# A four-layer hybrid decoder step on eight cores: three convolution heads ahead of v in the first pass, and five smaller reorderings

## What is computed

```python
for l in range(4):
    h = rmsnorm(x, pre_g[l])
    u, v, z_a, p, z_b, xc, bg, cg, z_c = split(h @ w_in[l])        # 1024 -> 6400 columns
    vn  = rmsnorm(v, v_g[l])                                       # A: chunks of 128, 6 heads
    a   = u * (tril(w_s[h]) @ vn + b_s)
    d   = trailing_mean(p, 2/4/8/16) - p                           # B: 4 groups of 128 channels
    b   = (d @ w_pg) * pool_scale
    c   = bg * conv3(cg * xc)                                      # C: depthwise, width 3, 6 heads
    mix = concat(a * silu(z_a), b * silu(z_b), c * silu(z_c))
    x   = x + rmsnorm(mix @ w_out[l], post_g[l])
```

## Time and profile before

| | us |
|---|---|
| median of 3 runs | 2166.12 |
| the three runs | 2033.6, 2166.12, 2173.4 |
| the profiled execution | 2033.48 |
| its span, slowest core | 2032.3 |
| spans of the eight cores | 2029.0 to 2032.3 |
| granted TensorE clock, mean | 0.996 to 0.999 |

### The profile page before, as it was taken

The page is one execution under the profiler, slowest core; times in us unless marked ns, Lnnn a source line. Parts: engine busy times, 40 slices in busy tenths (PEclk is TensorE's granted clock), DMA queues, the critical chain, the costliest instruction groups (busy, mean ns, idle before and its releaser), DMA issues.

```text
span 2032.3 us, 37323 instructions; the slowest of 8 cores (2029.0 to 2032.3 us)
## 1 busy us (share of the span) xinstructions
PE 2004.1 (99%) x12305; PEld 1185.9 (58%) x12305; DVE 1174.8 (58%) x1935; ACT 630.7 (31%) x1566; POOL 382.7 (19%) x752
## 2 busy tenths in 40 slices
PE   7999999999999999999999999999999999999998
PEld 4555565576566466557656546656755655664673
DVE  4654764575665475476575556547657544653763
ACT  4232332323323232232332332323333222231331
POOL 3211310221211120131131122013013111101300
PEclk9999999999999999999999999999999999999999
DMA  9999797689798875839969857595987974656662
GB/s 187 215 193 193 167 204 105 171 131 193 178 181 139 161 157 94 138 115 181 183 169 177 137 156 145 96 140 135 194 186 168 160 144 137 115 87 144 115 122 75
DMA packets 157099, 309.53 MB, mean 152 GB/s; under 512 B 78192, under 2 KB 83568, under 8 KB 155504
## 3 DMA queue, kind: packets, MB, share of 16 engines
q0 software_dynamic: 47376, 174.64, 54.5%
q1 hardware_dynamic: 109392, 132.25, 23.7%
q10 hardware_dynamic: 144, 0.26, 0.0%
HBM read 409.48 MB, written 55.99 MB: 229 GB/s over the span
## 4 chain that ended last, share of the span: by engine, by line
PE 93%; DMA 4%; DVE 1%; issue 1%; POOL 0%; SPq 0%; ACT 0%; DVEq 0%; POOLq 0%; ACTq 0%
PE ps L590 61%; PE ps L706 23%; PE ps L558 7%; DMA hd<-sb_hout 2%; DMA sb_b_bc<-b_sp 1%; PE ps L829 1%; DMA sb_ring<-w_in 1%; DMA sb_xs<-x_p 1%; PE ps L684 1%; PE ps L747 0%; DVE sb_pw L410 0%; DVE sb_mix L414 0%; POOL sb_stats L425 0%; DVE sb_vn L414 0%; ACT sb_scr L406 0%
## 5 line engine op out<-in xcount | busy, mean ns | idle before, releaser
L590 PE MATMUL ps<-sb_hT,sb_ring 128*128 128x384 bf16 (+1 forms) x8448 | 1324.7, 317 | 6.6 <-DVE sb_mix L414 3.0
L590 PEld LDWEIGHTS ps<-sb_hT,sb_ring 128*128 128x128 bf16 x8448 | 823.1, 98 | 471.6 <-issue 12.1
L406 ACT ACTIVATE sb_scr<-ps 128x384 f32<-128x384 f32 (+3 forms) x665 | 370.8, 562 | 1047.2 <-PE ps L590 494.2
L706 PE MATMUL ps<-sb_wout,sb_mix 128*128 128x512 bf16 x2144 | 464.7, 379 | 0.0
L706 PEld LDWEIGHTS ps<-sb_wout,sb_mix 128*128 128x128 bf16 x2144 | 209.9, 98 | 251.6
L356 POOL DMA_DIRECT2D sb_ring<-w_in x284 | 153.3, 543 | 973.1 <-PE ps L590 626.2
L414 DVE SCALAR_TENSOR_TENSOR sb_scr<-sb_pw,sb_convw,sb_scr 128x384 f32<-128x384 f32 (+1 forms) x336 | 182.0, 542 | 145.8 <-ACT sb_ccarry L406 109.5
L410 DVE TENSOR_TENSOR sb_scr<-ps,sb_scr 128x384 f32<-128x384 f32 (+1 forms) x288 | 151.8, 531 | 118.2 <-PE ps L829 91.4
L414 DVE SCALAR_TENSOR_TENSOR sb_hout<-sb_xs,sb_stats,sb_pre_bc 128x1024 bf16<-128x1024 f32 x62 | 79.6, 1285 | 189.3 <-POOL sb_stats L425 168.7
L558 PE MATMUL ps<-sb_ring,sb_hT 128*128 128x512 bf16 (+1 forms) x1088 | 178.8, 326 | 0.9 <-DMA sb_ring<-w_in 0.9
L410 DVE TENSOR_TENSOR sb_mix<-sb_scr 128x384 bf16<-128x384 f32 (+1 forms) x288 | 160.2, 556 | 30.7 <-DVE sb_scr L410 0.9
(11 more groups left out here) (55 smaller groups left out, 521.5 us busy)
## 6 DMA issues: line engine op xcount, KB each, us to landing
sb_ring<-w_in POOLq DMA_DIRECT2D x273, 512.0 KB, 10.9
xd<-sb_xs SPq DMA_DIRECT2D x51, 512.0 KB, 3.1
sb_xs<-xd SPq DMA_DIRECT2D x51, 512.0 KB, 11.8
sb_xs<-x_p SPq DMA_DIRECT2D x32, 512.0 KB, 15.2
sb_wout<-w_out POOLq DMA_DIRECT2D x32, 512.0 KB, 13.0
hd<-sb_hout SPq DMA_DIRECT2D x62, 256.0 KB, 4.2
sb_ring<-w_in POOLq DMA_DIRECT2D x11, 1024.0 KB, 9.9
y_p<-sb_xs SPq DMA_DIRECT2D x16, 512.0 KB, 2.9
```

Of the source, the lines that this page charges most:

```text
L406: return emit(ACT, lambda a: a.activation(out=out, in_=in_, func=func, scale=scale, **kw), reads=reads, writes=writes)
L590: ins = pe.matmul(bank(b, N), lhsT=wa.ap[:, k, :], rhs=hT[:, k, j0 * 128:j0 * 128 + N], start=(k == 0), stop=(k == 7))
L706: ins = pe.matmul(bank(b + half), lhsT=mix[:, k, j * 128:(j + 1) * 128], rhs=wout[:, k, half * 512:(half + 1) * 512], start=(k == 0), stop ...
```

## The change

1. Pass 0 runs convolution heads 0 to 2 (N_FRONT) ahead of v. Their six units move in the ring list behind p; w_sp, its mask product and the bias are handled in the hooks of these heads. SyncE no longer waits for v1. w_sp is staged in vn rows 4 and 5 rather than mix rows 10 and 11. The w_out pieces go to other hooks: heads 1 and 2 of the front, v tiles 3 and 5, a heads 1, 3, 5, and convolution head 3.
2. At the start the first weight unit is issued after the first norm, icnt, the setup constants and w_pg later. Rows 3 to 5 are copied to hT by VectorE. All pooling operations of pass 0 come after the front.
3. Next rows: in pass 0 the x tiles of pass 1 are asked for at v tiles 0 to 3 instead of 3 to 5, and hout has three buffers instead of two.
4. The bias table of the samples is gone; the operation repeats each of 8 values 16 times by its access pattern. b_bc is 3 KB a partition instead of 6, and the transfer half as large.
5. In the passes of group 2 the hooks take three pooling entries after v tiles 0 to 3, none after the last, none at head 0, two at the heads behind it.
6. In out_last each half's sum is waited for by its own token; eps is added to the first half's sum at once; sum and power follow.

```diff
-NHO = 2
+NHO = 3
...
+            if (g, l) == (0, 0):
+                k = len(units) - 12
+                units = units[:2] + units[k:k + 2 * N_FRONT] + units[2:k] + units[k + 2 * N_FRONT:]
+            pending.extend(units)
...
-            act(hT[:, :, j * 128:(j + 1) * 128], pb.rearrange("p (k t) -> p k t", k=8), AF.Copy,
-                reads=[bank_res[b]], writes=[R_hT[j]])
+            if on_dve:
+                dve_copy(hT[:, :, j * 128:(j + 1) * 128], pb.rearrange("p (k t) -> p k t", k=8),
+                         reads=[bank_res[b]], writes=[R_hT[j]])
...
-                dve_tt(scr[:, tm + half, :], bank(b + half), post_bc[:, half * 512:(half + 1) * 512], ALU.mult,
-                       reads=[bank_res[b + half], R_stat[sa[half]], R["post_bc"]], writes=[R_scr[tm + half]])
+                summed = R_stat[sa[half]].w
+                emit(DVE, lambda v, half=half: v.tensor_tensor(
+                    out=scr[:, tm + half, :], in0=bank(b + half), in1=post_bc[:, half * 512:(half + 1) * 512],
+                    op=ALU.mult),
+                     reads=[bank_res[b + half], R["post_bc"]], writes=[R_scr[tm + half]], extra=[summed])
+                if half == 0:
+                    emit(POOL, lambda q: q.tensor_scalar(out=c0, in0=c0, scalar1=EPS, scalar2=None, op0=ALU.add),
+                         reads=[R_stat[sa[0]]], writes=[R_stat[sa[0]]])
...
-                        bv = b_bc[:, k, h * 128:(h + 1) * 128]
+                        bv = b_bc[:, h * 128:(h + 1) * 128]
+                        if k == 1:
+                            bv = bv[:, 0:ST].unsqueeze(2).to_broadcast([128, ST, SB])
...
-                later_pop(2 if h == 0 else 3)
+                if g < 2:
+                    later_pop(2 if h == 0 else 3)
+                elif h > 0:
+                    later_pop(2)
...
-                ring_try_alloc()
                 warm_up()
                 nr(0)
+                ring_try_alloc()
                 nr(1)
-                ring_try_alloc()
                 sl.append(load_x(0, 4))
                 tj(0, 8)
                 nr(2)
-                load_wpg(0, 1, d_wpg[0])
                 ring_try_alloc()
...
-                v1 = W0["v1"].res[0].w
-                SP.h.wait_ge(*v1)
-                SP.waited[id(v1[0])] = v1[1]
-                setup_loads()
...
+                wo = list(range(8))
+
+                def hook(c):
+                    if c == 0:
+                        emit(SP, lambda q: q.dma_start(out=w32, in_=w_sp[0]), writes=R_w32, dsem=d_pw[1])
+                        load_b(0)
+                    else:
+                        wout_piece(l, wo.pop(0))
+                    if c == 1:
+                        dve_tt(wmt[:], w32.rearrange("p (a b) -> p a b", a=6),
+                               c32[:, C32_MASKP, :].unsqueeze(1).to_broadcast([128, 6, 128]), ALU.mult,
+                               reads=R_w32 + [R["c32"]], writes=[R["wmt"]])
+                c_phase(g, l, hook, 0, N_FRONT)
+                for gi in range(4):
+                    pool_vec(g, l, gi)
...
-                if j >= 3 or nt - j <= 3:
+                if (j < 4 if pi == 0 else j >= 3 or nt - j <= 3):
                     init_load()
-                later_pop(2 if g == 2 else 1)
+                if g < 2:
+                    later_pop(1)
+                elif j < nt - 1:
+                    later_pop(3)
...
-            c_phase(g, l, hook)
+            c_phase(g, l, hook, 0 if pi else N_FRONT)
```

More of the change, by code:

```diff
@@ L76 @@
 W_UNITS = _w_units()
+N_FRONT = 3
 W_ORDER = [s for u in W_UNITS for s in u]
@@ L175, in build_nc @@
     w_sm = din("w_sm", [DEPTH, 128, 6 * 128])
-    b_sp = din("b_sp", [DEPTH, 128, 2 * 768])
+    b_sp = din("b_sp", [DEPTH, 128, 768])
     w_pg = din("w_pg", [128, DEPTH * 4 * 128])
@@ L237, in build_nc @@
         vstage = sb("vstage", [128, WA], F32)
-        b_bc = sb("b_bc", [128, 2, 768], F32)
+        b_bc = sb("b_bc", [128, 768], F32)
         xs = sb("xs", [128, NX, D], F32)
@@ L388, in build_nc @@
             r0 = 0
+            units = []
             for names in W_UNITS:
@@ L398, in build_nc @@
                 u.slots = sum(x[2] for x in names) // 128
-                pending.append(u)
+                units.append(u)
+            if (g, l) == (0, 0):
+                k = len(units) - 12
+                units = units[:2] + units[k:k + 2 * N_FRONT] + units[2:k] + units[k + 2 * N_FRONT:]
+            pending.extend(units)
             wsched[(g, l)] = d
@@ L491, in load_b @@
         def load_b(l):
-            emit(SP, lambda q: q.dma_start(out=b_bc[:].rearrange("p a b -> p (a b)"), in_=b_sp[l]),
+            emit(SP, lambda q: q.dma_start(out=b_bc[:], in_=b_sp[l]),
                  writes=[R["b_bc"]], dsem=d_par["b"])
@@ L532, in norm_to_hd, with t_job @@
                  dsem=d_hout[o])
-        def t_job(j, s):
+        def t_job(j, s, on_dve=False):
             b = alloc_banks()
@@ L741, in out_last @@
             sa = [alloc_stat(), alloc_stat()]
+            c0 = stats[:, sa[0]:sa[0] + 1]
+            c1 = stats[:, sa[1]:sa[1] + 1]
             ju = alloc_scr()
@@ L857, in a_phase, with c_phase @@
                 hook(h)
-        def c_phase(g, l, hook):
+        def c_phase(g, l, hook, c0=0, c1=6):
             W = wsched[(g, l)]
             sts = GROUPS[g][1]
-            for c in range(6):
+            for c in range(c0, c1):
                 wzc = need(W[("zc", c)])
@@ L968, in run_pass @@
                 nr(2)
-                load_wpg(0, 1, d_wpg[0])
                 ring_try_alloc()
                 sl.append(load_x(0, 5))
+                emit(SP, lambda s_: s_.dma_start(out=icnt[:].rearrange("p a b -> p (a b)"), in_=icnt_d),
+                     writes=[R["icnt"]], dsem=d_icnt)
                 tj(1, 5)
@@ L975, in run_pass @@
                 tj(2, 4)
+                setup_loads()
                 load_vg(0)
@@ L982, in run_pass @@
                 pump()
+                load_wpg(0, 1, d_wpg[0])
                 pb_[1] = p_matmul(g, l, 1, 0)
@@ L992, in run_pass @@
                 for gi in range(4):
-                    pj(gi, 1)
+                    p_job(g, l, gi, 1)
                     release(wsched[(g, l)][("p", gi)])
-                    pool_vec(g, l, gi)
-                    later_pop(2 if gi else 0)
-                v1 = W0["v1"].res[0].w
-                SP.h.wait_ge(*v1)
-                SP.waited[id(v1[0])] = v1[1]
-                setup_loads()
[L1001 to L1004, removed]
+                w32 = vn[:, 4:6, :].rearrange("p k t -> p (k t)").bitcast(F32)
+                R_w32 = [R_vn[4], R_vn[5]]
+                wo = list(range(8))
[3 more added lines that the diff above has]
+                        load_b(0)
+                    else:
+                        wout_piece(l, wo.pop(0))
[5 more added lines that the diff above has]
+                for gi in range(4):
+                    pool_vec(g, l, gi)
             else:
@@ L1012, in run_pass @@
                 pool_phase(g, l, gmaj, hook)
-            wo = list(range(8)) if g == 0 else []
+            if pi:
+                wo = list(range(8)) if g == 0 else []
             init_t = list(GROUPS[pi + 1][0]) if pi < 2 else []
@@ L1054, in hook @@
                     wout_piece(l, wo.pop(0))
-                if c == 1 and (g == 0 or pi == 1) and l + 1 < DEPTH:
+                if c == (1 if pi else N_FRONT) and (g == 0 or pi == 1) and l + 1 < DEPTH:
                     load_pre(l + 1)
```

26 lines of the change are left out of this document (10 added, 16 removed).

## The result

The changed kernel takes 2051.59 us in the median of 6 runs. Against the kernel before the ratio is 1.0085, with a 95% interval of 1.0067 to 1.0103: slower by 0.85%, within the 2% that counts as the same. The profiled execution took 2051.04, its span is 2049.6, that of before 2032.3. The median of before, 2166.12 from three runs and 2100.84 from six, mixes runs near 2034 with runs in which one half of the chip ran at a lower clock, so it can't be set beside 2051.59; the ratio leaves those runs out.

A forecast was written before the change was run, and what follows sets the result against it. TensorE was busy 2004.1 of 2032.3 us, with DMA engines also full in the first pass. 2032.3 + 5.0 (first pass) + 11.7 (group 2) - 1.2 (tail) = 2047.8 span, given as 2050; own range 2042 to 2058, reaching to 2190.

The forecast's parts named there:

- The first pass: First pass: output projection starts 3.3 us later, waiting for w_out, plus 1.7 us of lower clock: +5.0 us.
- the group 2 passes: Passes 2, 5 and 8: 2.2 us net delay plus 1.7 us clock, 3.9 per pass, +11.7; last layer 0.
- what is given back in group 2: Head 0 of group 2: its pooling pair is gone, so the 0.73 us wait goes; net 2.9 - 0.7 = +2.2 us.
- The clock in group 2: Passes 2, 5, 8: lower TensorE clock after each 3.3 us wait, 1.7 us per pass, bounds 0 and 2.5.
- Last vn in group 2: Group 2 v phase: four more VectorE pooling operations ahead of the last vn delay it by 2.9 us.
- Last w_out piece: First pass: eighth piece, queued behind v0 and v1 of pass 1, lands at 172.0 instead of 163.2; bounds 168.5 and 177.
- The row transposes: Pass 1's transposes, issued up to 12 us sooner, hardly take any engine share; otherwise w_out lands nearer 177, sum 5 us higher.
- TensorE's arrival: First pass: TensorE reaches the output projection at 156.6 instead of 168.66, then waits 15 us for w_out.
- Clock behind the wait: Output projection of first pass: lower clock after the w_out wait costs 1.7 us, bounds 0 and 2.5.
- Tail: End of kernel: earlier eps and one operation fewer, -0.8 - 0.4 = -1.2 us; bounds -0.7 and -1.2.
- The range: Case as summed 2042 to 2058, chance 0.45; range reached to 2190 because two of three earlier times lay 6.5% higher.
- The intended gains of the first pass: Earlier start and 8.1 us of removed waits; w_out in time gives -12.1 (2033, chance 0.13); with group 2's gain 2018, 0.12.

The follow-up runs named there:

- the old hooks: Changed kernel with group 2's pooling hooks as before the change (two per v tile and at head 0, three at heads 1 and 2): span 2034.5 us, ratio 1.0011.
- the new hooks alone: Kernel before with only the new group 2 pooling hooks: span 2047.2 us, ratio 1.0077.
- norm elsewhere: Changed kernel with group 2's carried-over row norm run behind head 1 of the a phase instead of in the p phase: span 2036.7 us, ratio 1.0021.
- the run with the late piece: Kernel before with only pass 0's eighth w_out piece issued at convolution head 3 instead of 2: span 2041.1 us, timed runs 2041.73 and 2042.31.

## Why the total came out close, and which steps of the prediction failed

The cause, the places and the direction were as forecast: 2047.8 for the span, measured 2049.6, and +0.8% against 1.0085. That the total is so close is partly luck, as misses of opposite sign cancel. The first pass cost 3.8 us instead of 5.0, the group 2 passes 14.7 instead of 11.7. Point by point:

- **The step that failed: what is given back in group 2.** The prediction followed the list of 28 pooling entries only to the last vn, credited what head 0 no longer does, and put pass 11 at 0. What is pushed back it put at nothing without a reason. Head 3 now has two entries left, and its group matmul waits 1.39 us for them in all four passes of group 2, 5.6 us in all. Nearly all of the 1.6 us of pass 11 is this wait. The runs with the old hooks and with the new hooks alone show that the hooks bring it.
- **The clock in group 2.** 1.7 us were charged for each of three waits, 5.1 in all. The profiled core paid in passes 2 and 8 and not in pass 5, 2.7 us in all (13.1 measured, less three times 3.5 of waits). So the forecast of 11.7 was 3 x 2.2 + 3 x 1.7; the terms measured, 3 x 2.1 + 4 x 1.39 + 2.7, come to 14.6 of the 14.7. The overcharge of 2.4 us hid part of the missed 5.6.
- **Last vn in group 2.** Right: the job that needs it was to start 3.3 us late in one piece; measured is a wait of 2.61 us and, ahead of it, 0.60 for a vn write of the tile before, 3.2 in sum. Less the two old waits this is 2.1, forecast 2.2. Three runs show the mechanism (hooks out, hooks alone, norm elsewhere). The last of them shows that the late row norm, which the prediction named, is needed for it.
- **Last w_out piece.** Right that it comes late, and why: its place in the queue (moved ahead of v0 and v1 of pass 1 it gives 10 us; moved behind them in the old kernel it starts pass 1 5.2 us later on the profiled core, 7.4 in the mean of the eight). The landing was taken as 172.0, measured 169.4, nearer the low bound of 168.5. The saving of transfer work was sized too small. Packets and MB moved from the start to the landing of v1 of pass 1 before (173.3), then to that of the piece in the changed kernel (169.4):

```profile
DMA packets 11169, 33.73 MB, mean 195 GB/s; under 512 B 1918, under 2 KB 2174, under 8 KB 11026
q0 software_dynamic: 6494, 20.70, 76.7%
...
DMA packets 10878, 33.17 MB, mean 196 GB/s; under 512 B 1926, under 2 KB 2182, under 8 KB 10607
q0 software_dynamic: 6160, 20.52, 76.7%
```

  The software queue had moved nearly the same bytes, as the step assumed. In all it is 0.56 MB less, 2.9 us at 196 GB/s; the prediction had 0.39 MB at 275 GB/s, 1.4 us. The last 1 us lies within what the mean rate varies between runs (197 GB/s in the run with the late piece).
- **The row transposes.** The 3.9% of the earlier trace rows were read as their share, but the first of them was issued only at 163.7, late in that stretch of 25 us. The hardware queue from 165 to 170 us and from 170 to 175, before, then the same in the changed kernel:

```profile
q1 hardware_dynamic: 72, 0.02, 2.6%
q1 hardware_dynamic: 179, 0.05, 16.7%
...
q1 hardware_dynamic: 198, 0.05, 7.1%
q1 hardware_dynamic: 167, 0.04, 10.1%
```

  So in both kernels they get a share while the software queue is full, as they would by the Trainium skill (DMA: Bandwidth & Descriptors, section Queues, rings and completion order), which has each engine go round its queues packet by packet. The share is small: 7.1% of the last 5 us before the landing is 0.4 us, an estimate, and the bound of 177 that hung on it was not needed.
- **TensorE's arrival.** 156.6 forecast, 159.7 measured. The waits of 8.1 us went, but the ring brought new ones at the start (1.75 for the p units, 0.65 for v) and a wait for the VectorE row copy (0.94). All of it was hidden behind the w_out wait, as said: 9.9 us instead of 15.
- **Clock behind the wait.** 1.7 us forecast, 2.9 measured here, 1.5 to 2.9 over the cores. The price was taken from a wait of 2.16 us; after the one of 9.9 us the granted clock is 0.50 from 169 to 175. So the first pass is 0.9 us of later start and 2.9 of clock, where 3.3 and 1.7 were forecast.
- **Tail.** -1.2, measured -1.2.
- **The range.** 2042 to 2058 held the time. The upper end of 2190 stood for the level of the quoted median of before, 2166.12, for which no term of the sum accounts; 2050 was meant beside the 2033.5 of the profiled execution, and set beside that median it would read as a gain of 5%, which neither the sum nor the result says.

The intended gains of the first pass were real (some 6 us, once the piece is in time). With the eighth piece at head 5 and the hooks spread the kernel is 0.55% faster than before.

## What to carry to other kernels

Where a queue of transfers is always full, an edit that lets the engine arrive sooner is worth nothing if the last transfer needed now lands later: count what stands ahead of that transfer, before and after. A list of deferred operations has to be followed to its end: taking them sooner delays the result that shares their engine, taking fewer later leaves a rest ahead of its consumer. And a kernel whose matmul engine is 99% busy can still lose 17 us to a handful of waits, some of which are paid a second time in clock.

## What was not expected of the hardware

The price of a wait in clock varied: 1.7 us after 2.16 us at rest, nothing or some 1.3 to 1.7 us after the same 2.61 us, 1.5 to 2.9 us after 8.0 to 10.6 us. Filling the long wait with matmuls without use kept the projection at 41.6 us on all eight cores (granted clock 1.00 from 160 to 210 us on core 0), but brought no time. The cores differ by up to 4.4 us in the wait for a weight unit with the same program and data volume, and the slowest decides. So the effect of an edit at the edge of the transfers has to be read from all eight cores.
